# Up-projections of two convolutional feed-forwards: seven products of quarter blocks in place of eight

## What is computed

```python
def conv_ffn(h, w_up, w_dw, b_dw, w_down):
    u = causal_dwconv(h @ w_up, w_dw, b_dw)
    val, gt = jnp.split(u, 2, axis=-1)
    return (jax.nn.gelu(gt) * val) @ w_down
```

## Time and profile before

| what | value |
|---|---|
| median of 3 runs | 2243.86 us (2243.2 to 2246.38) |
| the profiled execution | 2245.13 us |
| its span in the trace | 2243.4 us |
| PE busy | 2192.8 us, 98% |
| POOL busy | 1213.1 us, 54% |
| DVE busy | 1147.4 us, 51% |
| ACT busy | 775.9 us, 35% |
| granted clock of TensorE, mean | 0.995 |

### The profile page before, as it was taken

One profiled execution on the slowest core, in us unless ns is written; L12 is line 12 of the kernel. 1 busy time (PEld: TensorE's weight loads), 2 busy tenths in 40 slices (PEclk: granted clock), 3 DMA queues, 4 the chain that ended last, 5 costly groups with the idle time before them and its releaser, 6 DMA issues.

```text
span 2243.4 us, 40182 instructions
## 1 busy us (share of the span) xinstructions
PE 2192.8 (98%) x16148; PEld 1726.6 (77%) x16148; DVE 1147.4 (51%) x1718; ACT 775.9 (35%) x1355; POOL 1213.1 (54%) x681
## 2 busy tenths in 40 slices
PE   9999999999999999988889999999999999999999
PEld 4867887888888667788877575668887788888887
DVE  7985547555520457754344526772227638555500
ACT  5464323333310266533324226770002242333200
POOL 1964454788877200000024454568887358777776
PEclk9999999999999999999999998999999999999999
DMA  8444652333223332220002240003334212332232
GB/s 333 160 141 151 215 187 94 110 101 93 95 97 98 111 114 76 76 80 5 5 4 94 76 164 7 2 11 94 100 98 136 88 47 94 94 102 94 93 95 102
DMA packets 65424, 220.75 MB, mean 98 GB/s; under 512 B 6913, under 2 KB 9226, under 8 KB 65282
## 3 DMA queue, kind: packets, MB, share of 16 engines
q1 hardware_dynamic: 51072, 179.81, 24.3%
q10 hardware_dynamic: 9986, 24.82, 3.1%
q0 software_dynamic: 4224, 14.06, 1.8%
HBM read 213.09 MB, written 11.86 MB: 100 GB/s over the span
## 4 chain that ended last, share of the span: by engine, by line
PE 77%; POOL 11%; issue 8%; DVE 3%; DMA 1%; ACT 1%; POOLq 0%; DVEq 0%; SPq 0%; ACTq 0%
PE banks L502 12%; PE banks L503 12%; PE banks L504 12%; POOL WH L451 5%; POOL WL_A L454 3%; PE banks L2124 3%; PE banks L2079 3%; PE banks L711 2%; PE banks L909 2%; PE banks L693 2%; PE banks L911 2%; PE banks L750 2%; PE banks L910 2%; PE banks L2395 2%; PE banks L2396 2%
## 5 line engine op out<-in xcount | busy, mean ns | idle before, releaser
L451 POOL TENSOR_TENSOR WH<-W,ZERO 128x1024 fp32r<-128x1024 f32 x194 | 368.5, 1900 | 277.8 <-PE banks L504 244.9
L454 POOL TENSOR_TENSOR WL_A<-W,WH 128x1024 fp32r<-128x1024 f32 x138 | 339.4, 2459 | 10.9
L502 PE MATMUL banks<-HF,WH 128*128 128x512 f32 x704 | 275.9, 392 | 0.1
L503 PE MATMUL banks<-HF,WH 128*128 128x512 f32 x704 | 274.0, 389 | 0.0
L504 PE MATMUL banks<-HF,WL_A 128*128 128x512 f32 x704 | 273.9, 389 | 0.0
L487 POOL TENSOR_TENSOR WH<-W,ZERO 128x1024 fp32r<-128x1024 f32 x19 | 39.4, 2073 | 270.9 <-PE banks L2124 188.8
L876 POOL TENSOR_TENSOR WR_LO<-W,FRONT_HI 128x1024 fp32r<-128x1024 f32 x40 | 97.6, 2446 | 119.3 <-ACT FRONT_HI L870 119.3
L502 PEld LDWEIGHTS banks<-HF,WH 128*128 128x128 f32 x704 | 132.1, 188 | 28.4 <-POOL WL_A L454 0.5
L503 PEld LDWEIGHTS banks<-HF,WH 128*128 128x128 f32 x704 | 132.2, 188 | 27.4 <-issue 0.2
L504 PEld LDWEIGHTS banks<-HF,WL_A 128*128 128x128 f32 x704 | 132.1, 188 | 27.4
L454 POOL TENSOR_TENSOR WL_C<-W,WH 128x1024 fp32r<-128x1024 f32 x56 | 141.7, 2531 | 4.4
(11 more groups left out here) (510 smaller groups left out, 5313.0 us busy)
## 6 DMA issues: line engine op xcount, KB each, us to landing
W<-stream SPq DMA_DIRECT2D x308, 512.0 KB, 3.5
BIG<-stream ACTq DMA_DIRECT2D x30, 512.0 KB, 4.9
BIG<-stream SPq DMA_DIRECT2D x20, 512.0 KB, 11.3
bias_rows<-bias_lines POOLq DMA_DIRECT2D x1, 4096.0 KB, 22.1
X<-x_t SPq DMA_DIRECT2D x2, 1024.0 KB, 7.5
BIG<-stream SPq DMA_DIRECT2D x2, 1024.0 KB, 11.7
bias_rows<-bias_lines POOLq DMA_DIRECT2D x1, 2048.0 KB, 16.0
BIG<-bias_rows POOLq DMA_DIRECT2D x1, 2048.0 KB, 11.5
```

Source lines behind the costliest of these rows:

```text
L451: nc.gpsimd.tensor_tensor(WH[:, half, :], W[:, slot, :], ZERO[:, 0:1].to_broadcast([P, D]), ALU.add)\
L454: nc.gpsimd.tensor_tensor(WL[stage][half], W[:, slot, :], WH[:, half, :], ALU.subtract)\
L502: nc.tensor.matmul(out_ap, w_hi, hi, start=start, stop=False)
L503: nc.tensor.matmul(out_ap, w_hi, lo, start=False, stop=False)
```

## The change

Two pairs of each up stage (`DIRECT`) stay as they were. For the other 20 (`SEVEN`) the pair's two units and the activations are cut into quarters: A11, A12 are the first unit's weights for the first and second 512 rows, A21, A22 those of the second unit; B11, B12 are the first four tiles of the activations at positions 0 to 255 and 256 to 511, B21, B22 the other four tiles. Strassen's method (Winograd's form) gives the four quarters of the result from seven products:

The sums of weights are made in place in `W` by POOL. The rounded copies of the seven quarters are now ACT's, into one of four slots of `OPERAND_HI`, and the rest is POOL's, into `OPERAND_LO`:

```diff
+        def pe_seven(pe, stage):
+            for p in range(SEVEN):
+                for s, (which, name) in enumerate(SEVEN_STEPS):
+                    pe.wait_ge(f_wlo, pool_at(stage, p, LOW_AT[s]))
...
+                    if s == 0 and p >= 2:
+                        pe.wait_ge(s_dve, dve_at(stage, p - 2, C21_AT[stage]))
...
+                    if s == 3:
+                        pe.wait_ge(s_tap, tap_at(stage, p, 1))
+                    if s in (4, 5, 6):
+                        pe.wait_ge(s_dve, dve_at(stage, p, s - 3))
...
+        def pool_seven(pool, stage):
+            for p in range(SEVEN):
+                a11, s2, s1, a12, s3, s4, a22 = (quarter(stage, p, s) for s in range(7))
+                def low(s):
+                    hi, lo = seven_weights(p, s)
+                    pool.wait_ge(f_whi, high_at(stage, p, s + 1))
+                    nc.gpsimd.tensor_tensor(lo, quarter(stage, p, s), hi, ALU.subtract).then_inc(f_wlo, 1)
...
+                nc.gpsimd.tensor_tensor(s1, s1, a22, ALU.add).then_inc(f_wlo, 1)
+                low(0)
...
+                nc.gpsimd.tensor_tensor(s2, s1, a11, ALU.subtract).then_inc(f_wlo, 1)
...
+                low(1)
+                low(2)
+                low(3)
...
+                nc.gpsimd.tensor_tensor(s3, a22, s2, ALU.subtract).then_inc(f_wlo, 1)
...
+                nc.gpsimd.tensor_tensor(s4, a12, s2, ALU.subtract).then_inc(f_wlo, 1)
...
+                low(4)
+                low(5)
+                low(6)
```

`high` on ACT waits for the product that used the slot three products earlier and for POOL's sum. The order on ACT of one pair, and the way the sums are prepared:

```diff
+            def high(p, s):
...
+                    act.wait_ge(*made(stage, *product_of(7 * p + s - 3)))
...
+                act.wait_ge(f_wlo, pool_at(stage, p, MADE_AT[s]))
+                nc.scalar.activation(seven_weights(p, s)[0], quarter(stage, p, s), ACT.Copy).then_inc(f_whi, 1)
...
+            for p in range(SEVEN):
+                n = p + DIRECT
+                high(p, 3)
+                if both and p:
+                    act.wait_ge(s_dve, dve_at(stage, p - 1, 8))
+                    last_tap(n - 1, 1, SQ[:, 3, :])
+                act.wait_ge(*made(stage, p, 1))
+                if p:
+                    act.wait_ge(s_dve, dve_at(stage, p - 1, C21_AT[stage]))
+                nc.scalar.activation(FIRST_PRODUCT, seven_bank(p, ALPHA), ACT.Copy).then_inc(s_tap, 1)
+                high(p, 4)
+                active(n - 1)
+                high(p, 5)
+                hidden_high(n - 1)
+                high(p, 6)
+                high(p + 1, 0)
+                high(p + 1, 1)
+                high(p + 1, 2)
+                act.wait_ge(s_dve, dve_at(stage, p, 6 if both else 7))
+                act.wait_ge(s_ev, base.ev + 2 * n)
+                last_tap(n, 0, SQ[:, 2, :])
...
+            act.dma_start(out_tiles, X[:]).then_inc(s_c, 16)
+            act.dma_start(rows[4:8].rearrange("h p m -> p h m"), H[:, 4:8, :]).then_inc(s_c, 16)
...
+            act_sums(act, "up1", plain)
             act_up(act, "up1", True)
+            act.wait_ge(*made("up1", SEVEN - 1, 7))
+            act.dma_start(X[:], out_tiles).then_inc(s_c, 16)
...
             dve.wait_ge(g_lo, DT)
+            dve_sums(dve, "up1")
             dve_up(dve, "up1", True)
```

More of the change, by code:

```diff
@@ L1574, in pe_up @@
                     unit(j, 0)
[L1575 to L1581, removed]
+            pe_seven(pe, stage)
+        PROD0, HIGH0, LOW0 = 2 * TAP_PAIRS, U0["mixo1"], U0["mixo1"]
+        ALPHA, BETA, GAMMA = range(3)
+        SEVEN_STEPS = [(ALPHA, "B11"), (BETA, "T2"), (GAMMA, "T1"), (ALPHA, "B21"), (BETA, "T3"), (ALPHA, "B22"), (BETA, "T4")]
@@ new lines, in taps, with whole, act_sums @@
+        def taps(name, j, t):
+            return PRM[:, C0[name] + 3 * j + t:C0[name] + 3 * j + t + 1]
+        def whole(part, n):
+            return part[:, 4 * n:4 * n + 4, :]
+        def act_sums(act, stage, plain):
+            for k in range(DT):
+                plain(k).then_inc(f_whi, 1)
+            for n in (1, 0, 2, 3):
+                act.wait_ge(s_dve, BASE[stage].dve + n + 1)
+                nc.scalar.activation(HR[:, 2 * n:2 * n + 2, :], X[:, 2 * n:2 * n + 2, :], ACT.Copy).then_inc(f_whi, 1)
@@ new lines, in last_tap, with direct @@
+            def last_tap(n, h, src):
+                c = C0[b] + FT * h + n
+                nc.scalar.activation(SQ[:, h, :], src, ACT.Identity, scale=taps(w, FT * h + n, 2), bias=PRM[:, c:c + 1])\
+                    .then_inc(s_tap, 1)
+            def direct(n, h):
+                if h == 0:
+                    act.wait_ge(s_ev, base.ev + 2 * n)
+                if both:
+                    act.wait_ge(unit_done, U0[stage] + 2 * n + h + 1)
+                else:
+                    act.wait_ge(g_t, 2 * DT + 2 * n + 1)
+                last_tap(n, h, psum[2 * n + h][:, :])
@@ new lines, in low, with added @@
+            def low(n):
+                dve.wait_ge(s_hi, base.prod + n + 1)
+                V.tensor_tensor(HIDS[1][:, n, :], SQ[:, 0, :], HIDS[0][:, n, :], ALU.subtract).then_inc(s_ev, 2)
+            first, second = slice(0, HALF_S), slice(HALF_S, S)
+            def added(p, product, which, to, other):
+                dve.wait_ge(*made(stage, p, product))
+                V.tensor_tensor(to, seven_bank(p, which), other, ALU.add).then_inc(s_dve, 1)
+            c11, c12, c21, c22 = SQ[:, 2, first], SQ[:, 2, second], SQ[:, 3, first], SQ[:, 3, second]
@@ new lines, in dve_up @@
+            for n in range(DIRECT):
+                nh = 2 if both else 1
+                if not both:
+                    scaled(n, 0)
+                for h in range(nh):
+                    dve.wait_ge(s_tap, base.tap + nh * n + h + 1)
+                    tap(n, h, psum[2 * n + h], s_dve, 1)
+                    dve.wait_ge(s_dve, base.dve + PARTED + nh * n + h + 1)
+                    if h < nh - 1:
+                        lag = 2
+                        V.scalar_tensor_tensor(SQ[:, h, lag:S], psum[2 * n + h][:, 0:S - lag], taps(w, FT * h + n, 0),
+                                               SQ[:, h, lag:S], ALU.mult, ALU.add)
+                    else:
+                        tap(n, h, psum[2 * n + h], s_conv, 0)
+                if not both:
+                    scaled(n, 1)
+                if n == 0:
+                    product(0)
+                    low(0)
@@ L1651, in pe_down @@
+            for p in range(SEVEN):
+                u2(p)
+                product(p + DIRECT - 1)
+                added(p, 4, ALPHA, c11, FIRST_PRODUCT)
+                low(p + DIRECT - 1)
+                rest(p)
+            product(FT - 1)
+            low(FT - 1)
         def pe_down(pe, stage, up):
@@ L3306, in _ @@
             split_weights(pool, "cao", 2, 8)
[L3307 to L3308 removed]
+            split_weights(pool, "up2", 0, 4)
+            pool_seven(pool, "up2")
+            pool_down(pool, "up2", "down2")
         @block.tensor
```

261 lines of the change are left out of this document (193 added, 68 removed).

## The result

The changed kernel takes 2571.33 us (median of 4 runs, 2569.14 to 2574.13) beside 2245.1 us for the kernel before on the same chip: a ratio of 1.1455, 95% interval 1.1435 to 1.1474, so 14.6% slower. The prediction had 2605 (2470 to 2690). The profiled execution took 2572.06 us, 327 more than the profiled one of before; 361 were forecast.

The account below looks back on a forecast made before the run. PE bounds the kernel now (98% busy); after the change, pairs' chains over POOL, ACT and DVE set the pace. 178 and 146 us for the stages, holes 34.5, ends 2: +361, median 2605 us, range 2470 to 2690.

Parts of the forecast that it names:

- first stage's cycle: First up stage: a pair's chain over POOL, ACT and DVE takes 19.8 us, against 10.88 before.
- That alone is above 10.88: POOL's eleven operations per pair, at 1.25 us plus hand-overs of 0.07, take 14.5 us, above the old pair's 10.88.
- 0.121 us for a matmul of 256 columns: PE in the changed pairs: assumed matmul time, making a product of quarters 1.45 us and a pair 10.2.
- fourth rival: PE's weight loads are not hidden behind 256 columns: 25 us a pair, 2845 us in all; chance 3%.
- third rival: PE's granted clock falls to 1.2 GHz as it idles: 19.1 us a pair on PE, 2641 us in all; chance 10%.
- Its two taps on DVE each wait for a POOL operation: 8.6 and 10.4: First-stage pair: the value half's two DVE taps, each held up by POOL, end 8.6 and 10.4 us after S1 starts.
- though POOL had been ready at 14.8: First-stage pair: POOL, ready at 14.8 us, waits for ACT's copy of S4 until 16.7 before making its low part.
- second stage's cycle, 18.2: Second up stage: a pair's chain over POOL, ACT and DVE takes 18.2 us, against 10.88 before.
- delays the next by about 0.5: Up-stage pairs: each DVE tap reading SBUF twice waits for POOL's current operation, then delays POOL's next by about 0.5 us.
- The port costs nothing: Rival: DVE's taps fall into POOL's own waits, so the chains shrink to POOL and ACT: 2481 us; chance 11%.
- The holes: PE idle at each stage's start during X's store, sums, low parts and direct units' work: 19 and 15.5 us.
- The 2 us at the ends: At the stage ends the first down unit waits for its split, about 1 us each, 2 us together.

Follow-up runs that it names:

- e10: Changed kernel with POOL's two waits for ACT removed and no DVE operation with both inputs in SBUF in the pairs (e6 and e7 together): 2411.7 us.
- e1: Changed kernel without the third pass (weights' low part by input's high part) of each product, 56 matmuls a pair in place of 84: 2565.2 us.
- e2: Changed kernel with ACT's last tap of the value half moved ahead of the copies of S2 and S1: 27 us less than the changed kernel.
- e6: Changed kernel with ACT's copy of A11 no longer waiting for S1 and the low part of S1 made ahead of that of S2: 2525.4 us.
- e7: e4 with gelu's result and the hidden product in PSUM too, so no DVE operation in the pairs has both inputs in SBUF: 2473.5 us.
- e4: Changed kernel with the finished quarters of the two halves put in PSUM banks 0 and 7 in place of SBUF: 2498.4 us.
- e8: Changed kernel with ACT's and DVE's work on each stage's first direct unit moved ahead of the sums T1 to T4, during X's store: 2561.3 us.
- e9: e6 with the last tap of the value half also moved ahead of the copies of S1 and S2, as in e2: 2504.5 us.

## Why the prediction was right

Right in sign, place and size: POOL's eleven operations take longer than PE's 10.88 us, whatever the others do. In the second stage the path that sets the period is the predicted one too; in the first the predicted path only ties with POOL's own work. The sum was 34 us too high, and 31 of these are one term, the first stage's cycle.

- **POOL against PE's gain.** "That alone is above 10.88": shown by e10, 14.06. The operation was taken at 1.25 and takes 1.27 to 1.30; eleven of them make 13.83 busy in e10 (248.86 over 18 pairs), near the 13.75, and the hand-overs only 0.24, where eleven of 0.07 had been added. An estimate from the Trainium skill (GPSIMD Engine Reference, 3.1) had been 1.35; the trace lies between.
- **PE.** 0.121 us for a matmul of 256 columns was 0.12 at the upper clock (562.14 and 562.26 below), and the loads were hidden: the fourth rival is out. The third rival's fall of the clock came in part (0.88 to 0.91 in the mean), and e1 shows that it had next to no price: with a third of the matmuls gone the periods are only 0.07 and 0.28 us shorter.

The timeline of PE in the first stage:

```profile
562.14 0.28 PE L1673 MATMUL banks<-XR,OPERAND_HI 128*128 128x256 f32 x1
562.26 0.28 PE L1674 MATMUL banks<-HR,OPERAND_LO 128*128 128x256 f32 x1
```

- **The first stage's cycle, 19.8: mis-sized.** The step that was off is "Its two taps on DVE each wait for a POOL operation: 8.6 and 10.4". Counted from S1 at 573.27, ACT's last tap ends at 6.67 (6.7 forecast), but the first tap runs at once, 0.75 instead of 1.9: it starts at 579.97, when POOL's operation in progress had about 0.15 us to go (578.85 and 1.27). Taps, gelu and the copy of S4 all come 1.2 to 1.7 us early (copy at 15.0, not 16.7). So "though POOL had been ready at 14.8" was right to 0.2 us, and next to nothing was left to wait for. 20 x (19.8 - 18.25) = 31. With that chain out of the way (e2) POOL's own work still takes 17.82, so the wrong step could cost no more than 2 us a pair. Where the first tap does meet POOL, in e6, the predicted wait appears with 1.8 us.
- **The second stage's cycle, 18.2:** measured 18.21, by the predicted path. The prediction has POOL end S4 at 13.4, after the copy of S3 at 12.25, and run on without a wait to 18.2; in the trace S4 ends at 13.2 and the last low part at 18.0 (S1 at 2312.77 above; other pairs take 18.3, with S2 lengthened too). e6 brings 1.62 here without any new wait, so POOL's work with its two waits and the meetings with DVE made that period.
- **The port.** "delays the next by about 0.5" measured about 0.4 in the mean (e7); "The port costs nothing", the second rival, is refuted by e4 and e7, 98 us together. POOL without gaps at 14 to 16 us, that rival's sign, came only in e10, where the meetings and the waits had been taken out.
- **The holes.** 19 and 15.5 forecast, 19.3 and 14.6 measured; the order store, sums, low parts, direct work was right as far as e8 tests it. The 2 us at the ends cannot be seen in the sum, which closes within 1 us without them.

## What to carry to other kernels

Fewer multiplications were worth nothing here, where preparing the operands fell to an engine that was already 79% busy: price the sums, splits and copies on their own engine before counting matmuls. Where operations of two engines lengthen each other over SBUF, one operand of each moved to PSUM can be worth more than a new order (98 us here, against 27 for the moved tap and 46 for the earlier copies). And when two chains are nearly as long as each other, shortening one shows the other: e6 gave 46 of 67 for that reason, and only all parts together (e10) gave the full sum.

## What was unexpected

- Taking a third of PE's matmuls away lowered the granted clock from 0.91 to 0.69 and from 0.88 to 0.74 (e1), so that PE's busy time fell by 9 and 16% only. Work left out of an engine that waits in every pair gave back less of its busy time here than its share.
- The price of a meeting depends on its phase: the same tap takes 0.75 or 1.66 us in the same pair, and with POOL's waits removed the same taps cost more (e9 got 0.98 of 1.8 us). A sum that charges each with a full wait is too high, one that charges none too low.
